# Input loading, input projection and a delta-rule recurrence in one block, and empty expert slots left out of gather and scatter

## The reference

```python
u = x @ w_in                            # 28 tiles of 128 columns
y_ssd   = _ssd_mixer(u_ssd, ...)        # 4 mixers, 256 columns each
y_rwkv  = _rwkv7_mixer(u_rwkv, ...)
y_gla   = _gla_mixer(u_gla, ...)
y_mlstm = _mlstm_mixer(u_mlstm, ...)
x = layer_norm(alpha * x + concat(y) @ w_out)
x = layer_norm(alpha * x + _moe_ffn(x) + per_layer_embedding)

def _rwkv7_mixer(u, ...):               # the delta rule, token by token
    u = u + (_token_shift(u) - u) * mu
    r, k, v, wd, ad, gd = _split(u, ...)
    # decay w, gate a, gate g from three small matrices; kk = k / |k|
    state = state * w + sa * b + v * k ;  o = state @ r
    return (group_norm(o) + bonus) * g

def _moe_ffn(x2d, ...):                 # 32 experts, each token goes to 4
    ...
```

## Time and profile before

| | |
|---|---|
| median of 3 runs | 4304.3 us (4297.6 to 4306.45) |
| the profiled execution | 4300.71 us, span 4299.0 us |
| mean granted PE clock | 0.894 of full speed |
| PE | 3661.8 us busy, 85% |
| PEld | 2902.2 us busy, 68% |
| DVE | 2605.5 us busy, 61% |
| ACT | 1932.6 us busy, 45% |
| POOL | 162.6 us busy, 4% |
| HBM traffic | 582.59 MB read, 26.80 MB written |

### The profile page before, as it was taken

How to read it: one execution, slowest core, us unless ns; L and a number is a source line. 1 busy time by engine, 2 the same in 40 slices (tenths; PEclk the granted TensorE clock), 3 DMA queues, 4 the chain that set the end, 5 groups by cost and what they waited for, 6 DMA issues and landing times. The chain is left out here.

```text
span 4299.0 us, 46714 instructions
## 1 busy us (share of the span) xinstructions
PE 3661.8 (85%) x16664; PEld 2902.2 (68%) x16664; DVE 2605.5 (61%) x3216; ACT 1932.6 (45%) x2319; POOL 162.6 (4%) x105
## 2 busy tenths in 40 slices
PE   7765367658999999999966899889999999889998
PEld 5622266546777777777755687667887777667887
DVE  2454632337899898998954576754652676645542
ACT  2121100116777777777742543543431543534432
POOL 0000000001111111111100000000000000000000
PEclk9875676758999999999988799988999899998998
DMA  3100000128999999999951111212332111112331
GB/s 135 49 1 0 1 0 1 39 87 332 357 360 363 351 351 353 360 356 345 356 199 50 66 54 51 69 44 68 98 102 73 66 54 59 50 45 83 98 102 60
DMA packets 112756, 611.42 MB, mean 142 GB/s; under 512 B 13426, under 2 KB 14722, under 8 KB 62658
## 3 DMA queue, kind: packets, MB, share of 16 engines
q1 hardware_dynamic: 102370, 575.36, 36.8%
q0 software_dynamic: 10240, 34.09, 3.1%
HBM read 582.59 MB, written 26.80 MB: 142 GB/s over the span
## 5 line engine op out<-in xcount | busy, mean ns | idle before, releaser
L1685 DVE TENSOR_TENSOR wl<-raw,wh 128x2048 fp32r<-128x2048 f32 x384 | 870.3, 2287 | 55.0 <-ACT wh L1639 54.8
L1639 ACT ACTIVATE wh<-raw 128x2048 fp32r<-128x2048 f32 x384 | 718.3, 1903 | 0.0
L1615 PE MATMUL pu<-wh,Xh 128*128 128x512 f32 x1024 | 405.9, 396 | 18.9 <-DVE wl L1685 18.7
L1617 PE MATMUL pu<-wh,Xl 128*128 128x512 f32 x1024 | 400.7, 391 | 0.0
L1616 PE MATMUL pu<-wl,Xh 128*128 128x512 f32 x1024 | 400.4, 391 | 0.0
L3230 DVE TENSOR_TENSOR w_low<-w_raw,w_high 128x1024 fp32r<-128x1024 f32 (+1 forms) x120 | 159.7, 1332 | 213.4 <-ACT w_high L3202 213.4
L3156 PE MATMUL ps<-x_high,w_high 128*128 128x512 f32 x704 | 280.7, 399 | 6.8 <-DVE x_low L508 6.1
L3157 PE MATMUL ps<-x_low,w_high 128*128 128x512 f32 x704 | 277.8, 395 | 0.0
L3202 ACT ACTIVATE w_high<-w_raw 128x1024 fp32r<-128x1024 f32 (+1 forms) x120 | 136.8, 1140 | 303.0 <-PE acc L3178 172.1
L2160 PE MATMUL acc<-x_high,w_high 128*128 128x512 f32 x576 | 249.0, 432 | 8.2 <-DVE x_low L508 6.2
L2745 DVE TENSOR_TENSOR w_low<-w_raw,w_high 128x1024 fp32r<-128x1024 f32 (+1 forms) x120 | 137.7, 1152 | 174.7 <-ACT w_high L2475 174.3
(11 more groups left out here) (608 smaller groups left out, 7268.7 us busy)
## 6 DMA issues: line engine op xcount, KB each, us to landing
raw<-in_exp_w SPq DMA_DIRECT2D x384, 1024.0 KB, 7.4
w_raw<-in_w_in SPq DMA_DIRECT2D x100, 512.0 KB, 3.4
w_raw<-in_w_up SPq DMA_DIRECT2D x88, 512.0 KB, 3.7
w_raw<-in_w_down SPq DMA_DIRECT2D x32, 704.0 KB, 4.0
w_raw<-in_w_out SPq DMA_DIRECT2D x32, 384.0 KB, 3.1
w_raw<-in_w_mem_kv SPq DMA_DIRECT2D x16, 512.0 KB, 4.0
w_raw<-in_w_out SPq DMA_DIRECT2D x8, 512.0 KB, 4.5
w_raw<-in_ple_gate_w SPq DMA_DIRECT2D x8, 512.0 KB, 4.5
```

The lines of the kernel that those rows point to most:

```text
L1615: nc.tensor.matmul(o, lh[:, k, :], wh[:, m % PARTS, c], start=(m >= 8 and kh == 0 and kk == 0), stop=False)
L1617: mm = nc.tensor.matmul(o, ll[:, k, :], wh[:, m % PARTS, c], start=False, stop=end)
L1639: nc.scalar.activation(wh[:, m % PARTS, :], raw[:, m % RAW, :], ACT.Copy).then_inc(w_high, 1)
L1685: nc.vector.tensor_tensor(wl[:, m % PARTS, :], raw[:, m % RAW, :], wh[:, m % PARTS, :], ALU.subtract).then_inc(w_low, 1)
```

## The change

`rwkv` and the calls that load and project are replaced by one function `opening`, called first. Its block holds everything from the loading of x to the last chunk of the recurrence. Its parts:

- SP issues the first half of x, the first weight tile, the second half of x, the second tile, then cols and the tables, in one row. The ring of `raw`, `wh` and `wl` has two buffers instead of four. The tiles come in another order (`IN_ORDER`): those of the delta rule first.
- ACT instead of DVE copies the banks to U.
- The elementwise work is put between the `wl` of tiles 2 to 13 on DVE; the gates, sums and transposes between the tiles on PE.
- The doubling rounds run beside tiles 14 to 27: half a tile on PE between `first(n+1)` and `second(n)`. DVE has `level(n+2)` behind the additions of round n.
- Only the product of b and a is made ahead of the doubling; the three other masked products are made per chunk within the recurrence, which also has two buffers for `started` and `sa`.
- No new big buffers: work data lies in x, y and free tiles of U. So x is overwritten, and `short_convs` loads it again (2 MB) beside the convolutions.
- The scans over 128 tokens (eight) become two over 512 with a mask, and 32 small instructions on the ends become four.

In the mixture gather and scatter get a bounds check: a slot whose row lies beyond 511 is left out. `rows` is cleared once beforehand.

```diff
-def short_convs(K, U, conv):
+def short_convs(K, U, conv, x, x_in):
+        @block.sync
+        def _(sp):
+            sp.dma_start(x[:, :, :], x_in).then_inc(x_back, 16)
+            sp.wait_ge(x_back, 16)
...
-def rwkv(K, U, lora, y):
+IN_ORDER = [LORA, K_, K_ + 1, R_, R_ + 1, V_, V_ + 1, NARROW] + list(range(0, 6)) + list(range(23, 27)) + list(range(13, 23))
+BEFORE = 13
+def opening(K, a, x, y, U, lora, gate_up):
...
+                def _(sp):
+                    sp.dma_start(x[:, 0:4, :], a["x"][:, 0:4, :]).then_inc(x_in0, 16)
+                    sp.dma_start(raw[:, 0, :], a["w_in"][IN_ORDER[0]]).then_inc(loaded[0], 16)
+                    sp.dma_start(x[:, 4:8, :], a["x"][:, 4:8, :]).then_inc(x_in1, 16)
+                    sp.dma_start(raw[:, 1, :], a["w_in"][IN_ORDER[1]]).then_inc(loaded[1], 16)
...
+                    for n in range(2, U_TILES):
+                        sp.wait_ge(low_ready, n - 1)
+                        sp.dma_start(raw[:, n % 2, :], a["w_in"][IN_ORDER[n]]).then_inc(loaded[n % 2], 16)
...
+                def _(pe):
...
+                    for n in range(3):
+                        tile(n)
+                    lora_products()
+                    tile(3)
+                    tile(4)
+                    kk_sums()
+                    for n in range(5, 10):
+                        tile(n)
+                    turn(0)
+                    turn(1)
+                    rk_sums()
+                    for n in range(10, BEFORE):
+                        tile(n)
+                    for n in range(2, 6):
+                        turn(n)
+                    tile(BEFORE, 0)
+                    for c in range(NT):
+                        pair(c)
+                    tile(BEFORE, 1)
+                    first(0)
+                    for n in range(NR):
+                        if n + 1 < NR:
+                            first(n + 1)
+                        tile(BEFORE + 1 + n // 2, n % 2)
+                        second(n)
+                    for q in range(3):
+                        products_of(0, q)
+                    for c in range(NT):
+                        right_side(c)
+                        if c + 1 < NT:
+                            products_of(c + 1, 0)
+                        solve(c)
+                        if c + 1 < NT:
+                            products_of(c + 1, 1)
+                        new_state(c)
+                        chunk(c)
+                        if c + 1 < NT:
+                            products_of(c + 1, 2)
...
+                def _(act):
...
+                    def after(n):
+                        act.wait_ge(product, n + 1)
...
+                        nc.scalar.activation(U[:, IN_ORDER[n], :], W[:, n % 2, :], ACT.Copy).then_inc(taken, 1)
+                        if n + 2 < U_TILES:
+                            high_part(n + 2)
...
+                def _(dve):
...
+                    def level(n):
+                        lv, c = ROUNDS[n]
+                        if n >= 2:
+                            dve.wait_ge(y_ready, n - 1)
+                        nc.vector.tensor_tensor(nm[:, n % 2, :, :], nt[:, c, :, :], spread(K.c("fwd", P, lv)), ALU.mult).then_inc(level_ready, 1)
...
+                    for n in range(NR):
+                        update(n)
+                        if n + 2 < NR:
+                            level(n + 2)
+                        if n % 2 and BEFORE + 3 + n // 2 < U_TILES:
+                            low_part(BEFORE + 3 + n // 2)
...
-                    pool.indirect_dma_start(rows[:, :], None, x_rows, bass.IndirectOffsetOnAxis(idx[:, odd:odd + 1], 0)).then_inc(gathered, 16)
+                    pool.indirect_dma_start(rows[:, :], None, x_rows, bass.IndirectOffsetOnAxis(idx[:, odd:odd + 1], 0),
+                                            bounds_check=S - 1, oob_is_err=False).then_inc(gathered, 16)
...
-                                            compute_op=ALU.add).then_inc(scattered, 16)
+                                            bounds_check=S - 1, oob_is_err=False, compute_op=ALU.add).then_inc(scattered, 16)
...
+                nc.vector.memset(rows[:, :], 0.0).then_inc(ones_ready, 1)
...
-            with parts_of(K, x) as (high, low):
-                project(K, a["w_in"], U_TILES, DT, high, low, S, U)
+            opening(K, a, x, y, U, lora, gate_up)
...
-            rwkv(K, U, lora, y[:, 2:4, :])
...
-        load(K, [(const[:, :], a["const"]), (cols[:, :], a["cols"]), (x[:, :, :], a["x"])])
```

More of the change, by code:

```diff
@@ new lines, in rk_sums, with turn @@
+                    def rk_sums():
+                        pe.wait_ge(rk, 2)
+                        pe.wait_ge(kk_root, 1)
+                        for t in range(2):
+                            mm = nc.tensor.matmul(G[:, t, :], K.c("sum64"), t1[:, t, :], start=True, stop=True)
+                        mm.then_inc(rk_sum, 1)
+                    def turn(n):
+                        if n < 2:
+                            pe.wait_ge(gates, 4)
+                            pe.wait_ge(mixed, 7)
+                        else:
+                            pe.wait_ge(keys_ready, 3)
+                            pe.wait_ge(g_taken, 1)
+                            if n >= 4:
+                                pe.wait_ge(taken_a if n % 2 else taken_v, n // 2 - 1)
+                        for j in range(NT):
+                            mm = nc.tensor.transpose(G[:, BANK[n], j * P:(j + 1) * P], items[n][0][:, j * P:(j + 1) * P], K.c("ident"))
+                        mm.then_inc(turned, 1)
@@ new lines, in first @@
+                    def first(n):
+                        lv, c = ROUNDS[n]
+                        pe.wait_ge(level_ready, n + 1)
+                        if lv:
+                            pe.wait_ge(x_ready, n - NT + 1)
+                        if n >= 2:
+                            pe.wait_ge(y_taken, n - 1)
+                        for h in range(H):
+                            mm = nc.tensor.matmul(py[n % 2][:, h, :], nm[:, n % 2, h, :], xi[:, c, h, :], start=True, stop=True)
+                        mm.then_inc(y_ready, 1)
@@ L1021, in _, with x_part @@
[L1021 to L1027, removed]
+                    def x_part(k):
+                        act.wait_ge(x_in1 if k >= 4 else x_in0, 16)
+                        nc.scalar.activation(high[:, k, :], x[:, k, :], ACT.Copy).then_inc(x_high, 1)
@@ new lines, in _ @@
+                    for k in range(4):
+                        x_part(k)
+                    high_part(0)
+                    for k in range(4, DT):
+                        x_part(k)
+                    high_part(1)
+                    after(0)
+                    lora_in()
+                    after(1)
+                    after(2)
+                    act.wait_ge(cols_in, 16)
+                    for f in range(2):
+                        for t in range(2):
+                            gate(f, t)
@@ L1030, in _ @@
                     act.wait_ge(diffs, 1)
-                    step.go(nc.scalar.activation(diff[:, 0:6, :], diff[:, 0:6, :], ACT.Exp))
-                    step.all()
+                    nc.scalar.activation(diff[:, 0:6, :], diff[:, 0:6, :], ACT.Exp).then_inc(exps, 1)
                     nc.scalar.activation(ends[:, :, :, :], ends[:, :, :, :], ACT.Exp).then_inc(exps, 1)
+                    after(9)
+                    turned_part(1)
+                    for n in range(10, BEFORE):
+                        after(n)
@@ new lines, in _ @@
+                    turned_part(2)
+                    turned_part(4)
+                    for c in range(NT):
+                        mask(c)
+                    dve.wait_ge(masked, NT)
+                    for c in range(NT):
+                        step.go(nc.vector.tensor_copy(xi[:, c, :, :], spread(K.c("ident"))))
+                    step.all()
+                    low_part(BEFORE + 1)
+                    level(0)
+                    level(1)
+                    low_part(BEFORE + 2)
```

600 lines of the change are left out of this document (342 added, 258 removed).

## The result

The median of four runs is 4177.99 us (4176.23 to 4182.39) against 4303.93 before: ratio 0.971, with a 95% interval of 0.9697 to 0.9723, so 126 us less where I forecast 107 and 4197 us. The profiled execution has a span of 4174.6 us.

A forecast was written before the change was run, and what follows sets the result against it. It took PE (85% busy) as the bound, no single stage dominating. Opening 429 against 514.3 us, 85 less, plus 22 in the mixture: 107 off the 4304.3 median, 4197 us; range 4155 to 4245, with 4183 to 4213 at chance 0.48.

The forecast's parts named there:

- The start: Opening's first loads: PE begins at 10.4 us instead of 31.79, with 8 and 15 as bounds.
- Tiles 0 to 13 and the fp32 pieces: Opening before the rounds: tiles, fp32 matmuls between them and waits, so that round 0 starts at 112 us.
- the 6 us of waits: Tiles 0 to 13: PE waits for late DVE work, low part 9, exponentials and rk sums; 6 us (0 to 20).
- the 79.0 and 16.2: Before round 0: 79.0 us for the tiles (8.3 + 13 x 5.44), 16.2 us for PE's other work between them.
- The 28 rounds: Doubling beside half tiles: the 2.26 us wait stays, each round takes 8.7 us, together 244 us (218 to 263).
- Rival 2: Doubling rounds: the clock stays full, 28 x 7.77 = 218 us, 26 us less, total 4171 us; chance 0.17.
- rival 4: Doubling rounds: the wait holds the clock at half, 13.3 us per round, 372 us, total 4325 us; chance 0.04.
- Rival 3: DVE or the two-deep ring late in tiles 0 to 13, or slow loading: 20 to 45 us more, about 4229; chance 0.14.
- Recurrence: End of the opening: hand-over and four chunks with products made per chunk, 71.5 us (66 to 78).
- x's second loading: Beside the convolutions: 2 MB take 7 us beside 20 us of convolutions, costing nothing unless over 20.
- The mixture: Gather and scatter with checks: landing 10.8 to about 7 us, DVE's wait gone, PE gains 22 us (0 to 29).
- the prediction's own sign of being wrong: Mixture: scatter landings still over 9 us would show the forecast wrong; near 7 us would show it right.

The follow-up runs named there:

- runs 4 and 5: Changed kernel; 4: DVE makes level(n+2) ahead of round n's additions, 4099.17 us; 5: PE runs the half tile ahead of first(n+1), 4092.33 us.
- run 8: Changed kernel with index(e+1) on DVE one chunk later, after chunk 5 instead of 4: 4153.46 us, ratio 0.9649.
- run 10: Changed kernel with index(e+1) on DVE after chunk 6 instead of 4: 4196.35 us, ratio 0.973.
- run 2: Kernel before with only the bounds checks on gather and scatter and the clearing of `rows`: 4283.67 us, ratio 0.9957.
- run 9: Kernel before with only the index moved behind chunk 5's low part, no bounds checks: 4260.03 us, ratio 0.9888.
- run 12: Kernel before, blocks separate, with level(n+2) ahead of round n's additions, the bounds checks, and the index behind chunk 5's low part: 4155.14 us, ratio 0.9646.

## Why the prediction was right, and where it was off

The direction and the range held, and so did the mechanism of the opening; that of the mixture did not. 4178 lies 19 us under the forecast, and below the 4183 to 4213 us that had the chance of 0.48. By the prediction's steps:

- **The start**: 9.23 us, forecast 10.4.
- **Tiles 0 to 13 and the fp32 pieces**: round 0 began at 103.05, forecast 112. The start gave 1.2 us of it. The term that failed is the 6 us of waits: from 9 to 103 us PE waited for nothing but 0.4 us for a mask, and 1.24 for the first level. DVE's list, walked, came out late where it was in time. That is 1.6 us for 6, so 4.4 us, and the remaining 3.4 are in the 79.0 and 16.2.
- **The 28 rounds**: the mechanism was right in each piece: the wait stays at 2.07 us (forecast 2.26), since `level(n+2)` stands behind the additions and the half tile behind the waiting `first`; runs 4 and 5 show it by removing it. The size was 235.5 us (103.05 to the end of the first addition at 338.50) for 244: the 26 rounds between the first and the last take 8.60 in the mean for 8.7, which gives 2.6 of the difference. The other 5.5 are the ends: the sum counts 28 full rounds, but from `first(0)` to the first addition it is 6.65 us, and the last round is 4.5 (28 x 8.7 is 243.6). The mean round before, 183.2/28 = 6.54, is misread in the same way: its window opens before the first round, and from the first to the last additions (536.31 to 707.75 us) 27 rounds take 6.35 each; no term of the sum uses it. Rival 2 (full clock throughout) holds for 13 of 26 rounds only, and rival 4 (13.3 us) is out. Rival 3 is out with the waits of tiles 0 to 13.
- **Recurrence**: 338.5 to 410.8, 72.3 us, forecast 71.5. The copy 1.2.
- **x's second loading** and everything between the opening and the mixture cost nothing that shows: ACT's first `x_high` before `w_out` (L240) moved from 798.61 to 697.33 us, 101.3, which is the opening's own gain to within a microsecond.
- **The mixture**: 21 us, forecast 22. The size was right by luck, the working was not: the prediction's own sign of being wrong, landings still over 9 us, came true. I took a landing of 7 us and a wait that vanishes, and it is 10.0 and a wait of 30.5 us. The landing fell by 0.8 us and POOL's instruction by 0.07 (2018 to 1947 ns), and as the waits were only 1.8 us each, that took 24 us off them. PE's waits for DVE's low part fell from 28.8 to 13.7 us, 15.1, not by 22. The rest of the 21 is a term that I did not have: PE's busy time fell by 5.3 us (1140.7 to 1135.4) at a granted clock of 1.00 both times; as in run 8 it went with the number of PE's waits.

What the prediction did not ask is what else could remove either wait. The answer, in a line or two each, is worth as much as the change: the mask's place 79 us on top of it (the tile's place 86) or 94 without it, the index's place 24 on top, or 41 to 49 without.

## What to carry to other kernels

Before filling an engine's idle time with other work, look at what ends the idle time: an instruction that two engines' lists merely put in the wrong order costs nothing to move, and the filler, placed behind the waiting instruction, fills nothing. Count a short wait on a busy PE as more than its length: here a recorded 2.07 us cost 2.39 at full clock, and in the mixture waits of 15.2 us in sum were worth 24.3 (run 8). Now and then the clock falls behind one too, which cost 1.6 us in every second round of the opening and followed 5 of 24 waits in run 10. And when a DMA is late, try the later place of the instruction that waits for it before making the DMA smaller.

## What was not expected of the hardware

- **A skipped row is still a packet.** q0 has 10240 packets with and without the check, and with the check alone (run 2) the packets under 512 B rose from 13426 to 17522, by 4096, which is 64 for each of the 64 gathers and scatters, the number of empty slots. Half the bytes brought the scatter's median landing from 10.8 to 10.0 us. Over all traces it is 10.8 to 11.4 us without the check and 9.2 to 10.7 with it, so the two nearly meet (10.8 in run 9, 10.7 in run 12). Halving the bytes does not halve that landing; what sets it wasn't measured.
- **The clock in the recurrence.** PE is busy there for 20.00 of 20 us, with its small fp32 matmuls (L1173, L1174) back to back, at a granted 0.50, the 1.2 GHz level. The doubling of run 12, as busy and fp32 too, has 1.00. Why the one is held and the other not stays open.
- **POOL beside DVE.** The gather instruction takes 2.28 or 1.21 us by what DVE runs next to it (run 10). In the changed kernel a low part runs from 1503.11 to 1505.40 us and the gather from 1504.03 to 1506.32, so it ends 0.9 us after the low part. By the Trainium skill, SBUF — State Buffer, section SBUF: two separate sides, an instruction of DVE with two SBUF inputs, as the low part is, and one of GpSimd that reads SBUF exclude each other for the whole instruction. Runs 8 and 10 fit that, with 1.1 us of difference, where the low part still had 1.4 us to run when the gather's instruction began; that the two SBUF inputs are the cause was not tested by itself. It can matter only where the gather is waited for, and what it is worth there wasn't measured.
